# Two of four down projections as seven block products, feed-forward weight sums made in memory, and a weight ring

## The reference, cut to what matters

```
def finish_layer(x, a, b, ga, gb, w_a, w_b, w_o, g1, b1, w_up, w_down, g2, b2):
    mix = (ga * (a @ w_a) + gb * (b @ w_b)) @ w_o
    x = layer_norm(ALPHA * x + mix, g1, b1)
    h = jnp.square(jax.nn.relu(x @ w_up)) @ w_down      # (640 x 1024)(1024 x 4096), (640 x 4096)(4096 x 1024)
    return layer_norm(ALPHA * x + h, g2, b2)
```

## Time and profile before

| | |
|---|---|
| median of 3 runs | 2148.25 us (2148.22 to 2148.42) |
| span of the profiled execution | 2145.2 us |
| TensorE busy | 2134.6 us |
| VectorE busy | 1469.7 us |
| ScalarE busy | 1182.0 us |
| GpSimd busy | 0.2 us |
| moved by DMA | 268.19 MB, mean 125 GB/s |

### The profile page before, as it was taken

One profiled execution on the slowest core, in us unless ns is written; L12 is line 12 of the kernel. 1 busy time (PEld: TensorE's weight loads), 2 busy tenths in 40 slices (PEclk: granted clock), 3 DMA queues, 4 the chain that ended last, 5 costly groups with the idle time before them and its releaser, 6 DMA issues.

```text
span 2145.2 us, 38346 instructions
## 1 busy us (share of the span) xinstructions
PE 2134.6 (100%) x15100; PEld 1950.9 (91%) x15100; DVE 1469.7 (69%) x2420; ACT 1182.0 (55%) x2513; POOL 0.2 (0%) x4
## 2 busy tenths in 40 slices
PE   9999999999999999999999999999999999999998
PEld 7998889999989898989889888899999898989897
DVE  6757778677879373636667577786769793646466
ACT  4457776686625362627234677766865262627261
POOL 0000000000000000000000000000000000000000
PEclk9999999999999999999999999999999999999999
DMA  5367562421341222212333765525113412212231
GB/s 190 103 250 256 210 235 89 160 98 51 108 162 41 98 86 72 89 69 89 108 110 103 276 249 202 203 93 179 60 60 108 152 60 79 89 69 91 78 108 69
DMA packets 68162, 268.19 MB, mean 125 GB/s; under 512 B 10984, under 2 KB 12648, under 8 KB 61296
## 3 DMA queue, kind: packets, MB, share of 16 engines
q1 hardware_dynamic: 43136, 152.75, 20.2%
q10 hardware_dynamic: 24848, 112.99, 14.8%
HBM read 236.35 MB, written 25.95 MB: 122 GB/s over the span
## 4 chain that ended last, share of the span: by engine, by line
PE 98%; ACT 1%; DVE 0%; DMA 0%; issue 0%; DVEq 0%; ACTq 0%
PE PS L719 10%; PE PS L721 10%; PE PS L720 10%; PE PS L649 9%; PE PS L651 9%; PE PS L650 9%; PE PS L617 9%; PE PS L619 9%; PE PS L618 9%; PE PS L847 2%; PE PS L872 2%; PE PS L810 1%; PE PS L760 1%; PE PS L861 1%; PE PS L792 1%; PE PS L990 1%
## 5 line engine op out<-in xcount | busy, mean ns | idle before, releaser
L2133 DVE TENSOR_TENSOR w_lo<-w_raw,w_hi 128x1024 fp32r<-128x1024 f32 x178 | 215.9, 1222 | 243.9 <-ACT w_hi L1245 235.1
L617 PE MATMUL PS<-xt_hi,w_hi 128*128 128x320 f32 x1184 | 382.2, 323 | 0.3
L619 PE MATMUL PS<-xt_hi,w_lo 128*128 128x320 f32 x1184 | 365.7, 309 | 0.0
L618 PE MATMUL PS<-xt_lo,w_hi 128*128 128x320 f32 x1184 | 365.4, 309 | 0.0
L1245 ACT ACTIVATE w_hi<-w_raw 128x1024 fp32r<-128x1024 f32 x178 | 186.6, 1058 | 303.9 <-PE PS L721 284.2
L719 PE MATMUL PS<-w_hi,act_a_hi 128*128 128x512 f32 x800 | 312.3, 390 | 0.0
L720 PE MATMUL PS<-w_lo,act_a_hi 128*128 128x512 f32 x800 | 311.4, 389 | 0.0
L721 PE MATMUL PS<-w_hi,act_a_lo 128*128 128x512 f32 x800 | 311.4, 389 | 0.0
L617 PEld LDWEIGHTS PS<-xt_hi,w_hi 128*128 128x128 f32 x1184 | 222.7, 188 | 5.6 <-issue 4.3
L618 PEld LDWEIGHTS PS<-xt_lo,w_hi 128*128 128x128 f32 x1184 | 223.0, 188 | 0.1
L619 PEld LDWEIGHTS PS<-xt_hi,w_lo 128*128 128x128 f32 x1184 | 222.3, 188 | 0.0
(11 more groups left out here) (338 smaller groups left out, 4770.6 us busy)
## 6 DMA issues: line engine op xcount, KB each, us to landing
w_raw<-in_weights SPq DMA_DIRECT2D x274, 512.0 KB, 3.5
kc<-in_k_cache ACTq DMA_DIRECT2D x32, 1024.0 KB, 7.9
vc<-in_v_cache ACTq DMA_DIRECT2D x16, 2048.0 KB, 8.7
gates_kept<-a_t ACTq DMA_DIRECT2D x8, 640.0 KB, 6.9
k_out<-k_t ACTq DMA_DIRECT2D x16, 320.0 KB, 2.4
v_out<-rows ACTq DMA_DIRECT2D x2, 2560.0 KB, 16.8
mix_a<-a_t ACTq DMA_DIRECT2D x2, 2560.0 KB, 12.2
rope_c<-gates_kept ACTq DMA_DIRECT2D x10, 320.0 KB, 3.1
```

The lines of the kernel that those rows point to most:

```text
L617: mm(out, wh, hi[:, k, c], start=(k == 0), stop=False)
L618: mm(out, wh, lo[:, k, c], start=False, stop=False)
L619: last = mm(out, wl, hi[:, k, c], start=False, stop=(k == KT - 1))
L2133: v.tensor_tensor(w_lo[slot][:], raw[:, raw_of(s, n)[0], :], w_hi[slot][:].bitcast(F32), ALU.subtract)\
```

## The change

The change touches the feed-forward block and what feeds it.

- **Down projections of parts 1 and 2** (`BLOCK_PARTS`) are made by `block_down` as seven block products: output rows in tiles (0, 2) and (1, 3), hidden features in even and odd tiles, output columns in two halves. Row tile 4 is multiplied undivided. Eight weight operands (four blocks, four sums) of two chunks each are used, with 3, 2, 2, 3, 2, 1, 3 and 2 output tiles. VectorE makes four sums of each activation pair (`act_sums`, 256 columns each), ScalarE and VectorE split them in five steps (`sum_high`, `sum_low`), ScalarE copies banks three times (`block_seed`), and VectorE takes nine results (`block_take`).
- **Weight sums** for the feed-forward block no longer come from VectorE. GpSimd issues transfers from memory to memory, some of which add to their destination, and leaves the sums in two new tensors `up_sums` and `down_sums`. There are six jobs a layer of eight transfers each; a full job has transfers of 1 MB, that of part 0's ups 512 KB. Layer by layer they start when `w_ready` of the last gate pair rises; SP waits for a job before it loads its first sum.
- **Weight ring.** Up pairs (after the plain ones) and block down projections take their weights from a ring of four `w_hi`/`w_lo` slots (`RING`), four chunks a pair (three of 1024 columns, one of 512) and 16 a block down projection. `ring_high` and `ring_low` make the parts; semaphores `ring_hi`, `ring_ready`, `ring_done` order them.
- Some semaphores are merged to make room, the sign of one activation sum and of two copies changes, the SBUF arena grows from 212480 to 225088 bytes and the scratch for GpSimd's descriptors is set to 4096.

The core of the diff:

```diff
+BLOCK_PARTS = (1, 2)
+PAIR_RING, BLOCK_RING = 4, 16
...
+        RING = (8, 7, 0, 1)
...
+        @block.gpsimd
+        def _(pool):
...
+            def put(dst, src):
+                pool.dma_start(dst, src).then_inc(sum_dma, 16)
+
+            def add(dst, src):
+                pool.dma_start(dst, src, accum_op=ALU.add, max_dma_last_dim=8 * D).then_inc(sum_dma, 16)
+
+            def up_sums_of(l, part, before):
...
+                put(s1, a21)
+                put(s3, a11)
+                pool.wait_ge(sum_dma, 16 * (before + 2))
+                add(s1, a22)
+                add(s3, a21)
+                pool.wait_ge(sum_dma, 16 * (before + 4))
+                put(s2, s1)
+                pool.wait_ge(sum_dma, 16 * (before + 5))
+                add(s2, a11)
+                pool.wait_ge(sum_dma, 16 * (before + 6))
+                put(s4, s2)
+                pool.wait_ge(sum_dma, 16 * (before + 7))
+                add(s4, a12)
+                pool.wait_ge(sum_dma, 16 * (before + 8))
...
+            for j, (l, kind, part) in enumerate(SUM_JOBS):
+                if part == 0:
+                    pool.wait_ge(w_ready[0], nth(l, AT_HEADS) + 1)
+                (up_sums_of if kind == "up" else down_sums_of)(l, part, JOB_TRANSFERS * j)
```

TensorE's block down projection:

```diff
+                def operand(o, outs, start, ready):
+                    for u in range(FF_PAIRS):
+                        slot, c = RING[(g + 2 * o + u // 2) % RING_SLOTS], u % 2 * BANK
+                        if u % 2 == 0:
+                            pe.wait_ge(ring_ready, g + 2 * o + u // 2 + 1)
+                        ready(u)
...
+                            mm(out, xh, wh, start=start and u == 0, stop=False, skip_group_check=True)
+                            mm(out, xh, wl, start=False, stop=False, skip_group_check=True)
+                            last = mm(out, xl, wh, start=False, stop=(u == FF_PAIRS - 1), skip_group_check=True)
...
+                operand(1, [(6, sum_tile(1, 0), lambda: pe.wait_ge(p5_copied, q + 1)),
+                            (7, sum_tile(1, 1), lambda: pe.wait_ge(up_taken, 2 * q + 2))], True,
+                        lambda u: u % 2 == 0 and pe.wait_ge(s_lo_ready, 5 * d + 1 + u // 2))
```

ScalarE's ring copy and its list for an up pair:

```diff
+            def ring_high(g):
+                j, loads = raw_of_ring(g)
+                act.wait_ge(raw_loaded[j], 16 * loads)
+                if g >= RING_SLOTS:
+                    act.wait_ge(ring_done, g - RING_SLOTS + 1)
...
+                fn(w_hi[RING[slot]][:, c], raw[:, j, c], ACT.Copy).then_inc(ring_hi, 1)
...
+            def up_pair(l, part, u):
...
+                if not first:
                     up_square(l, part, u - 1, 0)
                     up_relu(l, part, u - 1, 1, 0)
+                    next_high(l, part, u - 1, 3)
+                if not begun:
+                    ff_seed(l, part, u, 0)
+                if not first:
                     up_square_high(l, part, u - 1, 1)
                     up_square(l, part, u - 1, 1)
+                if not begun:
+                    ff_fifth(l, part, u)
+                next_high(l, part, u, 0)
+                if not begun:
+                    ff_seed(l, part, u, 1)
                 up_relu(l, part, u, 0, 0)
+                next_high(l, part, u, 1)
+                ff_seed(l, part, u, 2)
                 up_relu(l, part, u, 1, 1)
+                next_high(l, part, u, 2)
                 up_relu(l, part, u, 0, 1)
                 up_square_high(l, part, u, 0)
```

VectorE's list for an up pair (`ff_add` is the add of `p5`; 1 is the odd tile, 0 the even one):

```diff
+            def up_pair(l, part, u):
+                block = part in BLOCK_PARTS
+                if u > first_pair(part):
                     up_low(l, part, u - 1, 0)
+                    next_low(l, part, u - 1, 3)
                     up_low(l, part, u - 1, 1)
+                    if block:
+                        act_sums(l, part, u - 1)
+                next_low(l, part, u, 0)
+                next_low(l, part, u, 1)
+                ff_add(l, part, u, 1)
+                next_low(l, part, u, 2)
+                ff_add(l, part, u, 0)
+                if u == FF_PAIRS - 1:
                     up_low(l, part, u, 0)
+                    next_low(l, part, u, 3)
                     up_low(l, part, u, 1)
+                    if block:
+                        act_sums(l, part, u)
```

More of the change, by code:

```diff
@@ L707, in row_group @@
                     slot = LAST_ROWS[k // 2] if between is not None else s
+                    if first_slot is not None and k < 2:
+                        slot = first_slot
                     if between and (r, k) in between:
@@ L1925, in combined_pair @@
-                if u > first:
                     up_square(l, part, u - 1, 1)
-                if not begun and not second:
-                    up_fifth(l, part, u)
-                if not last:
-                    part_highs(l, part, u + 1, (1,))
-                else:
-                    high(0, down, skipped=1)
-                if not begun and not second:
-                    up_seed(l, part, u, 1)
-                if not last and not begun:
-                    part_highs(l, part, u + 1, (2,))
+                if not begun:
+                    ff_fifth(l, part, u)
@@ new lines, in block_down, with lows, takes @@
+            def block_down(l, part):
+                g = ring_block(l, part)
+                def lows(first, end):
+                    for c in range(first, end):
+                        ring_low(g + c)
+                def takes(*which):
+                    for i in which:
+                        block_take(l, part, i)
+                sum_low(l, part, 0)
+                sum_low(l, part, 1)
+                lows(4, 5)
+                sum_low(l, part, 2)
+                lows(5, 6)
+                takes(0, 1)
+                lows(6, 8)
+                sum_low(l, part, 3)
+                lows(8, 11)
+                sum_low(l, part, 4)
+                takes(2, 3)
+                lows(11, 13)
+                lows(13, 14)
+                takes(4)
+                lows(14, 17)
+                takes(5, 6)
+                lows(17, 19)
+                takes(7, 8)
+                lows(19, 20)
@@ L3094, in stream, with blocks @@
         out += row_form(w_o[l])
+        out += feature_tiles(w_up[l], range(2 * PLAIN_PAIRS))
         for part in range(FF_PARTS):
-            out += feature_tiles(w_up[l], range(part * KT, (part + 1) * KT))
-            out += row_form(w_down[l][part * D:(part + 1) * D])
+            if part not in BLOCK_PARTS:
+                out += row_form(w_down[l][part * D:(part + 1) * D])
     return np.ascontiguousarray(np.stack(out))
+def blocks(w_up, w_down):
+    import numpy as np
+    up = w_up.reshape(DEPTH, 2, KH, P, FF_PARTS * FF_PAIRS, 2, P).transpose(0, 5, 1, 4, 3, 2, 6)
+    up = up.reshape(DEPTH, 4, FF_PARTS * FF_PAIRS, P, BANK)
+    tiles = [part * FF_PAIRS + u for part, u in UP_ORDER]
+    first, count = BLOCK_PARTS[0], len(BLOCK_PARTS)
+    down = w_down[:, first * D:(first + count) * D].reshape(DEPTH, count, 2, 2, 2, P, 2, BANK)
+    down = down.transpose(0, 1, 4, 6, 2, 5, 3, 7).reshape(DEPTH, count, 4, 2, P, D)
+    return np.ascontiguousarray(up[:, :, tiles]), np.ascontiguousarray(down)
 def tables():
@@ L3175 @@
     keep = CHUNK * 2 - DEC_T
+    up_blocks, down_blocks = blocks(w_up, w_down)
     arrays = {
```

738 lines of the change are left out of this document (510 added, 228 removed).

## The result

The changed kernel took 2202.47 us (median of 4 runs, 2198.75 to 2204.85) where the kernel before took 2148.32 beside it (4 runs): ratio 1.0251, 95% interval 1.0237 to 1.0266, 54 us slower. The forecast was 2151, its range 2129 to 2162: wrong.

The account below looks back on a forecast made before the run. TensorE's own instruction order was taken as the bound, busy 2134.6 of 2145.2 us. Terms -21.8 + 18.6 + 3.0 + 3.0 = +2.8 gave 2148.0; with the runs' median 3.05 above the span, 2151 us, range 2129 to 2162.

Parts of the forecast that it names:

- Saving: Down projections of two parts in two layers: 96 fewer matmuls on TensorE at 0.2268 us each, -21.8 us.
- Late seed copy: Up pairs: ScalarE's copy of product 0 ends after product 2 is due, 1.06 or 0.84 us a pair, +18.6 us.
- operand 1: Start of four block down projections: the second operand waits for the first sum's low, 0.75 us each, +3.0 us.
- rival A: Up pairs: the seed copy isn't late, so the saving and a little contention remain, 2129 to 2140 us; 28%.
- Weight sums off VectorE: Feed-forward block: fewer sums and lows on VectorE, which was no bound, so 0 us.
- the block's ring: Block down projections: weight chunks come in time through the four slots, so no cost in the sum.
- rival C: Block down projections: the weight ring starves, 2 to 3 us in four blocks, 2156 to 2162 us; 8%.
- Adding transfers: First head: GpSimd's transfers delay the second half of `kc`, 1.5 us a layer, +3 us; bounds 0 and +6 a layer.
- Rival B: Sums late, or head loads starved: `kc` 6 us late in both layers and some later head, 2157 to 2165; 17%.
- Sums in time: Feed-forward block: a full job takes 87 us, five and a half 480 us, done before parts 1 and 3 want them.

Follow-up runs that it names:

- the floor: Changed kernel without GpSimd's transfers, plain blocks loaded instead, and VectorE's even add ahead of the third weight chunk's low: 2127.91 us, ratio 0.9905.
- the swap: In up pairs of the changed kernel, VectorE's even add goes ahead of the third weight chunk's low: 2186.76 us; without GpSimd's transfers 2127.91 against 2150.2.
- the last experiment: Changed kernel with even add first, 2 KB rows, and each layer's six jobs released in four places of that layer: 2135.11 us, ratio 0.9936.
- the spread version: Changed kernel, even add first, jobs released in four places, some layer 1 jobs in layer 0's feed-forward: 2148.76 us with 2 KB rows, 2171.57 with 8 KB.

## Why the prediction was wrong

*Saving, -21.8 us: right.* Measured -20 (the floor against before), 96 matmuls fewer as counted; 10.6 in the feed-forward part of layer 0, half of it.

*Late seed copy, +18.6, and operand 1, +3.0: right.* 20 waits, 0.7 us each in parts 1 and 2 and 0.9 in parts 0 and 3 (0.66 and 0.88 predicted), 0.92 with the restart in a pair of part 1 (0.84 predicted), none at a part's first pair; four of 0.4 us at operand 1. Together 21.6 predicted, 22.6 measured by the swap. The cause is the order of two instructions in VectorE's list, as given; the swap removes all of them. So rival A, the copy not late, was wrong of this kernel but is what the swap makes of it.

*Weight sums off VectorE, 0, and the block's ring, 0 (rival C): right.* Without transfers no wait on a block's weights is left.

*Adding transfers, +3 with bounds of 0 to +12: this step failed.* It measured 52 us. The term was built from one load, the second half of the first `kc`, with "later heads load `kc` and `vc` most of a head ahead of their use". (The issue that it reads from the earlier trace rows has a row of its own at the same time, `117.14 0.36 ACTq L1304 DMA_DIRECT2D kc<-in_k_cache  x1`. Its own figures, 5.5 less 1 less 3.3, give 1.2, where it takes 1.5.) That half of `kc` was late by 5.0 and 5.6 us in the two layers, within the bound of 6. The rest was cut off with that one sentence. The jobs ran without a pause from 114 to about 505 us, so the heads, the branch and the beginning of the window attention all had them beside their loads; the share of the 16 engines rose to 0.96. Two places that the prediction had not looked at gave way. In the heads behind the first, ScalarE was held by the issue of a load (4.49 us), and no `kc` or `vc` came late: from one head's first `kc` matmul to the next the changed kernel needs 34.65 us once, at the late `kc`, and 32.43 once, at that issue, where the kernel before needs 27.17 and 27.48 at these places: 12.4 us. The other 12 of the layer are lost in the branch, where ScalarE waited for kept gates and its bank copies came behind them. Late weights were not the cause: a chunk landed in 10.5 us instead of 5.9, but from 120 to 483 us ScalarE waited for one only once, 1.4 us.

A check that was to be had: the kernel before used 0.59 of the engines from 128 to 350, which leaves 91 us of all engines. By the prediction's own upper prices, 5.5 us of all engines for a copy of 1 MB and 11 for an add, one full job asks for 66, and some three ran in that stretch. The measured price is half of that (q0's 16.3% of 2203 us is 359 us for 11 full jobs' worth, 33 each), and it still filled the engines. So every stage behind the first head had to be looked at, and not one load's slack. Rival B had the mechanism (starved loads) but priced `kc` alone, late in both layers and one more head: 2157 to 2165.

*Second part of the miss: the price of a wait.* The changed kernel's waits add up to 56.5 us in the wait view, those without transfers to 19.5. The difference of 37.0 stands against one of 54.3 between the two profiled spans: 1.5 us for each us waited. At the first head it can be followed: of 7.48 us lost 5.02 are the wait, and the 2.46 left are what some 5 us at half the clock cost. Over the whole execution the mean granted clock was 0.991 for 0.999, an estimated 18 us of clock for the 17 that are left; some of it falls into the waits themselves, so that it makes up all of the difference is not shown. The seed waits of 0.7 us don't bring the clock down (window 640 to 1166 above, granted clock 1.00).

*Sums in time: right.* SP never waited for `sum_dma`. A full job took 60 to 80 us in the changed kernel (the first 167.0 to 246.9) and 436.6 to 498.2 = 61.6 us beside window attention in the last experiment, against 87 predicted. The Trainium skill, "DMA: Bandwidth & Descriptors", section "Anatomy of one DMA", whose fit made it an estimated 35, is too low for these jobs of copies and adds from memory to memory.

The same page, section "Queues, rings and completion order", says that each DMA engine takes turns between its queues, a packet at a time. Its packet is typically of 9 to 17 descriptors; whether the profile counts the same packets is not shown. Such turns would fit the row size: with rows a quarter as long the adds took more engine time and yet the kernel lost 12 us less (23 in the spread version), as if the loads had their turn sooner. No run here shows the turns themselves, nor whether the 16 engines or the memory behind them were the narrow place; and the cheap plain copies in pieces of 30 KB are not explained by it.

## What to carry to other kernels

A transfer that nobody waits for is not free: hold it against the free DMA share of every stage that it runs through, over its whole length, and there against the load, or the issue of a load, with the least slack; start it by gates where both leave room. When the wait view names an engine that is half idle, read what held that engine. Then look at what is queued just ahead of the instruction that releases TensorE: one low part moved behind one add was worth more (22.6 us) than the 96 matmuls saved (20). Short rows in a background transfer that adds are worth trying; the rows of the loads themselves were not varied here.

## What the runs showed that was not expected

- The cost of the adding transfers depended on their rows' length more than on their engine time: 8 KB to 2 KB gave 12 and 23 us back while q0's share of the engines rose from 16.3% to 17.9%.
- The same 92.28 MB cost 52 us behind one gate a layer and, with shorter rows, at most 7 us in four places.
- Around a wait of 5.02 us the granted clock was at half from 134 to 140 us, 5 us of it with TensorE back at work (0.74 over the 9 us behind the wait); after waits of 0.7 us it stayed at 1.00.
- Beside the transfers the issue of one `kc` load held ScalarE for 4.49 us; in the kernel before no such issue took more than 0.91.
